# A hybrid DeltaNet and RG-LRU layer on one core: one convolution of the last rest as products on TensorE, the output tiles' third load moved into the last scan, the opening on four strips

## The reference, cut to what matters

```python
shift, scale, gate = split(silu(c) @ ada_w + ada_b)          # the "mod" row, 3 x 1024, one for prompt, one for sample
h    = rmsnorm(x, pre_w) * (1 + scale) + shift
proj = h @ w_in                                              # q, k, v, z, beta, a, rx, rg
q, k, v = silu(short_conv(qkv, conv_w))                      # 4 taps along the tokens
o    = gated_delta(q, k, v, g, beta, s0)                     # both directions, chunks of 64, 8 heads of 128
o    = rmsnorm(o_f + flip(o_b), norm_w) * silu(z)
xf   = short_conv(rx, conv_w) + conv_b                       # 8 blocks of 128
r, i = sigmoid(xf @ w_r + b_r), sigmoid(xf @ w_i + b_i)
y_rg = (scan(a, bx) + flip(scan(a, bx))) * silu(rg)
y    = concat(o, y_rg) @ w_out                               # 1152 x 2048 @ 2048 x 1024
out  = x + gate * rmsnorm(y, post_w)                         # also the final states of the prompt
```

## Time and profile before

| | |
|---|---|
| Time, median of 3 runs | 1277.43 us (1277.24 to 1278.47) |
| The profiled execution | 1277.96 us, of which the span of the trace is 1276.3 us |
| PE busy | 1200.8 us, 94% of the span, 8626 instructions |
| DVE busy | 988.7 us, 77% |
| ACT busy | 727.7 us, 57% |
| POOL busy | 134.5 us, 11% |
| Mean granted TensorE clock | 0.983 of full speed (1.2 and 2.4 GHz are its two levels) |
| Costliest group | the projection's products L800 to L802, 1176 each, 428.5, 397.5 and 397.8 us of busy PE |
| Output products | L1165, 756 in all, 297 us |

### The profile page before, as it was taken

One profiled execution on the slowest core, in us unless ns is written; L12 is line 12 of the kernel. 1 busy time (PEld: TensorE's weight loads), 2 busy tenths in 40 slices (PEclk: granted clock), 3 DMA queues, 4 the chain that ended last, 5 costly groups with the idle time before them and its releaser, 6 DMA issues.

```text
span 1276.3 us, 23925 instructions
## 1 busy us (share of the span) xinstructions
PE 1200.8 (94%) x8626; PEld 1070.7 (84%) x8626; DVE 988.7 (77%) x2033; ACT 727.7 (57%) x1721; POOL 134.5 (11%) x138
## 2 busy tenths in 40 slices
PE   5999999999999999999999999999998698499997
PEld 2699989998999899899989998998898375288885
DVE  5774998999899989999998999898999757422221
ACT  4745487648665874777486658656775736111110
POOL 4000010101010100011010101000100000412120
PEclk9999999999999999999999999999999799799999
DMA  8522111112011211211121112112112902443330
GB/s 292 167 59 72 34 60 47 37 52 80 26 52 58 67 36 41 87 30 53 52 76 30 52 39 86 36 34 64 60 52 82 380 22 83 136 122 101 107 115 33
DMA packets 96431, 99.25 MB, mean 78 GB/s; under 512 B 4497, under 2 KB 79522, under 8 KB 96322
## 3 DMA queue, kind: packets, MB, share of 16 engines
q1 hardware_dynamic: 93378, 87.33, 22.3%
q0 software_dynamic: 2944, 10.49, 2.2%
HBM read 82.50 MB, written 15.30 MB: 77 GB/s over the span
## 4 chain that ended last, share of the span: by engine, by line
PE 48%; DVE 34%; issue 10%; ACT 5%; DMA 1%; DVEq 1%; SPq 0%; POOL 0%; ACTq 0%; POOLq 0%
PE bank L1165 12%; DVE arena L1938 6%; DVE arena L1936 6%; PE bank L800 5%; PE bank L801 5%; PE bank L802 5%; DVE arena L1777 4%; PE bank L1025 3%; DVE w_lo L1656 2%; DVE arena L1903 2%; PE bank L1139 2%; PE bank L1151 2%; PE bank L1072 2%; PE bank L1112 2%; PE bank L1121 2%
## 5 line engine op out<-in xcount | busy, mean ns | idle before, releaser
L800 PE MATMUL bank<-hT_hi,w_hi 128*128 128x384 f32 (+1 forms) x1176 | 428.5, 364 | 1.8 <-DVE w_lo L1656 1.2
L802 PE MATMUL bank<-hT_hi,w_lo 128*128 128x384 f32 (+1 forms) x1176 | 397.8, 338 | 0.0
L801 PE MATMUL bank<-hT_lo,w_hi 128*128 128x384 f32 (+1 forms) x1176 | 397.5, 338 | 0.0
L800 PEld LDWEIGHTS bank<-hT_hi,w_hi 128*128 128x128 f32 x1176 | 222.2, 189 | 11.1 <-DVE w_lo L1656 2.7
L801 PEld LDWEIGHTS bank<-hT_lo,w_hi 128*128 128x128 f32 x1176 | 222.2, 189 | 5.1
L802 PEld LDWEIGHTS bank<-hT_hi,w_lo 128*128 128x128 f32 x1176 | 221.2, 188 | 0.0
L1777 DVE SCALAR_TENSOR_TENSOR arena<-arena 128x1154 f32<-128x1154 f32 x96 | 141.1, 1470 | 5.2 <-DVE arena L1777 2.8
L1520 ACT ACTIVATE arena<-bank,arena 128x128 f32<-128x128 f32 x272 | 78.2, 370 | 104.2 <-PE bank L1129 104.2
L1165 PE MATMUL bank<-wo_hi,ot_hi 128*128 128x512 f32 x252 | 99.8, 396 | 22.5 <-DVE ot_lo L2145 16.7
L1165 PE MATMUL bank<-wo_hi,ot_lo 128*128 128x512 f32 x252 | 98.6, 391 | 0.0
L1165 PE MATMUL bank<-wo_lo,ot_hi 128*128 128x512 f32 x252 | 98.6, 391 | 0.0
(11 more groups left out here) (246 smaller groups left out, 2223.7 us busy)
## 6 DMA issues: line engine op xcount, KB each, us to landing
w_raw<-w_in SPq DMA_DIRECT2D x49, 512.0 KB, 4.0
arena<-scr_G SPq DMA_DIRECT2D x16, 576.0 KB, 4.7
arena<-x_sample SPq DMA_DIRECT2D x16, 512.0 KB, 7.6
arena<-ada_w SPq DMA_DIRECT2D x16, 512.0 KB, 10.9
wo<-w_out SPq DMA_DIRECT2D x4, 2048.0 KB, 13.0
ot<-scr_o SPq DMA_DIRECT2D x7, 1024.0 KB, 6.5
scr_o<-arena POOLq DMA_DIRECT2D x8, 576.0 KB, 3.7
scr_o<-arena POOLq DMA_DIRECT2D x8, 512.0 KB, 2.9
```

Source lines behind the costliest of these rows:

```text
L800: pe.matmul(out, w_hi[:, slot, k], hT_hi[:, k, cols], start=first, stop=False)
L801: pe.matmul(out, w_hi[:, slot, k], hT_lo[:, k, cols], start=False, stop=False)
L802: return pe.matmul(out, w_lo[:, slot, k], hT_hi[:, k, cols], start=False, stop=last)
```

## The change

Five things are done at once.

1. **Opening.** `ada_rows` writes four strips of 256 columns (output partitions 0, 32, 64 and 96) for each k instead of two of 512. DVE and ACT copy two strips each, the transposes use four banks with one more wait (`mod_turned` 6), and `make_mod` has five DVE instructions where it had three. Two of POOL's clears (`sub[0]`, `Z`) now stand behind `baT_made`.
2. **Gate row.** The norm weight is loaded beside the gate row in four small loads and multiplied into it by DVE at step 1 of the last scan (four multiplications of 2 rows x 256). POOL's two multiplications of 128 x 1024 and a load of 512 KB go.
3. **Heads.** The backward scan over the samples runs as one instruction (step 6). The first tap of xf goes from DVE (step 7) to ACT (step 6, Identity with scale and bias); DVE's taps 1 and 2 stand at steps 7 and 8. The two silus stand at steps 5 and 7.
4. **Last rest.** ACT makes four diagonal matrices of v's taps, and PE convolves v by 12 fp32 products in banks 2 to 4; ACT takes the silu from PSUM in three pieces. DVE's three taps go. The norm of o is done by nine ACT copies instead of one DVE instruction, and `turn_o` stands ahead of v's products.
5. **Output.** Tile 2's rows are loaded in the last scan behind tile 1's, its last head's rows with those of tiles 0 and 1, into the space that held tile 0's high part (`ot_raw`, `ot_high` and `ot_low` rotate three buffers). Its high and low part stand ahead of `y_tile(0, 0)`. `raw_last(0)` comes one k earlier, and DVE's copy of the states stands behind its last two `low_wo` instead of ahead of them.

```diff
 def load_o_rows(tile, first, n):
+    to, done = ((ot[:, 0], ot_in[0]), (ot[:, 1], ot_in[1]), (ot_raw[0], ot_next_in))[tile]
...
             load_o_rows(1, 0, HEADS - 1)
+            load_o_rows(2, 0, HEADS - 1)
...
             load_o_rows(1, HEADS - 1, 1)
+            load_o_rows(2, HEADS - 1, 1)
...
-            sp.dma_start(post_b, post_norm_w.to_broadcast([P, D])).then_inc(post_in, 16)
...
             sp.wait_ge(y_made, 1)
             sp.dma_start(y_prompt[0], y_out[:, 0]).then_inc(y_stored[0], 16)
-            load_o(0, 2)
...
-            for s in range(2):
-                gp.tensor_tensor(gate_post[:, s], gate_post[:, s], post_b, ALU.mult).then_inc(gate_post_made, 1)
...
-                for n in range(2):
-                    j = 2 * n + half
-                    mm = pe.matmul(banks[0][32 * j:32 * j + 2, :], silu_c[:, :, k], adaw[:, half, k, 512 * n:512 * n + 512],
+                for j in range(4):
+                    mm = pe.matmul(banks[0][32 * j:32 * j + 2, 0:256], silu_c[:, :, k], adaw[:, half, k, 256 * j:256 * j + 256],
...
+                    project(IN_SCAN + 8, 64 - IN_SCAN, b)
+                    pe.wait_ge(scores_taken.sem, scores_taken.next(b, 28))
+                    turn_o(b)
+                    pe.wait_ge(turn_taken.sem, turn_taken.next(b, 12))
+                    pe.wait_ge(proj_taken.sem, proj_taken.at(b, 6))
+                    pe.wait_ge(conv_done.sem, conv_done.at(b, 3))
+                    pe.wait_ge(v_begun.sem, v_begun.next(b, 4))
+                    for g, (o, n) in enumerate(GROUPS):
+                        for t in range(4):
+                            mm = pe.matmul(banks[2 + g][:, 0:n], v_diag[:, t], raw[:, 1, o + t:o + t + n],
+                                           start=(t == 0), stop=(t == 3))
+                    mm.then_inc(conv_done.sem, 1)
+                    project(72, 16, b)
...
                         if last and step == 1:
-                            pe.wait_ge(gate_row_made, 4)
+                            pe.wait_ge(gate_summed, 4)
...
-                    for k in range(16):
-                        mm = out_product(buf, half, k, k == 0, k == 15)
+                    for k in K_ORDER:
+                        if half == 0 and k == K_LAST[0]:
+                            pe.wait_ge(wo_hi_made, 16)
+                            pe.wait_ge(wo_lo_made, 16)
+                        mm = out_product(buf, half, k, k == K_ORDER[0], k == K_ORDER[-1])
...
-                if i == 10:
+                if i == 9:
                     raw_last(0)
...
+                if final:
+                    act.wait_ge(o_meaned.sem, o_meaned.at(b, 2))
+                    for ch in range(NCH):
+                        last_o = act.activation(o_tok[:, ch], o_tok[:, ch], ACT.Copy, scale=hcc["rstd"][:, ch:ch + 1])
...
-                    if step in (5, 6) and not last:
-                        x = (sz, sg)[step - 5]
+                    if step in (5, 7) and not last:
+                        x = sg if step == 5 else sz
...
+                    if step == 6 and not last:
...
+                        act.activation(xf, raw[:, 0, 0:TW], ACT.Identity, bias=colsB[:, bd(B_CB + b + 1, 1)],
+                                       scale=rconvw[:, 0, bd(b + 1, 1)]).then_inc(xf_begun.sem, 1)
...
-            act.wait_ge(gate_post_made, 2)
+            high_part(0, 2, 64)
             y_tile(0, 0)
-            high_part(0, 2, 80)
...
-                                  (slice(TW - 1, MID - 1, -1), colsB[:, bd(B_ST + 8 + b, 1)]),
-                                  (slice(MID - 1, P + GAP - 1, -1), RC[:, MID:MID + 1]))[d]
+                                  (slice(TW - 1, P + GAP - 1, -1), colsB[:, bd(B_ST + 8 + b, 1)]))[d]
...
-            TAPS = [[], [(1, 0)], [(1, 1)], [(1, 2)], [(1, 3)], [], [], [(2, 0)], [(2, 1)]]
+            TAPS = [[], [(1, 0)], [(1, 1)], [(1, 2)], [(1, 3)], [], [], [(2, 1)], [(2, 2)]]
...
+                    if step == 1 and last:
+                        for j, (row, post) in enumerate(zip(gate_rows, post_rows)):
+                            dve.wait_ge(gate_summed, j + 1)
+                            dve.tensor_tensor(row, row, post, ALU.mult).then_inc(gate_row_made, 1)
...
-            for i in range(5, 12):
-                low_wo(i)
-            dve.wait_ge(states_turned, 1)
-            dve.tensor_copy(hc[0:16, 0:P], banks[7][0:16, 0:P]).then_inc(states_taken, 1)
-            for i in range(12, 14):
+            for i in range(5, 14):
                 low_wo(i)
...
-            dve.wait_ge(gate_post_made, 2)
+            low_part(0, 2)
+            dve.wait_ge(post_in, 16 * 4)
             y_tile(0, 0, 0)
             for i in range(14, 16):
                 low_wo(i)
-            low_part(0, 2)
+            dve.wait_ge(states_turned, 1)
+            dve.tensor_copy(hc[0:16, 0:P], banks[7][0:16, 0:P]).then_inc(states_taken, 1)
             y_tile(1, 1, 1)
```

178 lines of the change are left out of this document (103 added, 75 removed).

## The result

| | before | after |
|---|---|---|
| Time, median | 1277.34 us (1277.10 to 1278.47) | 1256.12 us (1255.92 to 1257.22), 4 runs each |
| Ratio | | 0.9834 (95%: 0.9821 to 0.9846) |
| Span of the trace | 1276.3 us | 1254.3 us |
| PE busy | 1200.8 us, 94% | 1199.7 us, 96% |

The change makes the kernel 21.2 us faster by the medians. PE's busy time is nearly the same in sum: the strips shorten `ada_rows` from 14.8 to 9.2 us, and v's products add 7.9. So what is gained in all came out of waits. I tracked it by the start of the same PE instruction in both traces: each term is the shift that builds up across its stretch.

A forecast was written before the change was run, and what follows sets the result against it. PE, busy 94% of the span, was taken as the bound, so savings count where it waits. Opening -2.0, gate row 0, heads -0.6, last rest +4.0 and output -19.5 sum to -18.1: 1259.3 us, range 1250 to 1266.

The forecast's parts named there:

- What bounds the kernel: Whole kernel: PE is full nearly everywhere, so savings count where PE waits; the chain's 34% for DVE doesn't describe the heads.
- Opening, -2.0: Opening: four strips shorten `ada_rows`, cut short by the last load's landing at 47.3 to 49.2; -2.0 us, bounds -3.4 and -1.
- Gate row, 0: Last scan: DVE's four multiplications and SP's row stores cost nothing; 0 us, POOL's saved 6.16 us counted in the output.
- Heads, -0.6: Seven heads: DVE's lighter step 7 gains only tenths, -0.1 us each; -0.6 us, bounds -6 and +2.4.
- the 0.4 that the prediction named as its own limit: Inner heads: the forecast is wrong if heads differ from 118.36 us by over 0.4 us.
- step 6 loses what step 7 wins, because the longer backward scan stands there in one piece: Heads: the one-piece scan at step 6 cancels step 7's gain from losing the 0.88 us tap; -0.1 us per head taken.
- The statement on the joins: Head joins: relieving DVE gains only tenths at PE's 0.40 us wait, since DVE then waits 0.50 us for ACT's scaling of q.
- Last rest, +4.0: Last rest: v's products delay the gate products and ACT's chain behind them by 7.7 us; +4.0 us, bounds -3.4 and +6.
- The rival in which DVE bounds the last rest: Last rest: DVE's release decides, giving -3.4 us instead of +4; 1251.9 us, chance 0.15.
- Output, -19.5: Output: the 16.70 us wait before tile 2, 1.6 ahead of it and 1.2 of restart go; -19.5 us, bounds -20.5 and -13.
- The slack at `y_made` 1: Output: `y_made` 1 ends near 1094.4, about 1 us before PE needs it; the shared port could use that up.
- The sum: Whole kernel: -2.0 + 0 - 0.6 + 4.0 - 19.5 = -18.1 us, from 1277.43 to 1259.3 us, chance 0.58.

The follow-up runs named there:

- the run with the late load: Changed kernel with tile 2 loaded behind `y_made` 1 again and its high and low parts behind the first `y_tile`: 1272.54 us.

## Why the prediction was right, and where it was wrong

- **What bounds the kernel.** Right in the main: what is gained in all came from PE's waits, with PE's busy time 1.1 us less, and the chain's 34% for DVE were no measure of the heads. But the small waits in the heads were worth more than the prediction gave them.
- **Opening, -2.0.** Right in mechanism: the landing is the bound (48.1, between the 47.3 and 49.2 of the prediction). The products end 2.98 us earlier (2.3 forecast), at 49.17 instead of 52.15, of which 0.40 are lost again by 75.61 (0.3 forecast). The four strips do run side by side (1.05 us for two k). The run with two strips gives the part 2.9 us. One sum is wrong without effect: 3.4 us is four times 0.84, the gain of one half's eight k, and both halves would give 6.7 if PE alone decided.
- **Gate row, 0.** Right for the row itself; its worth is in the output.
- **Heads, -0.6.** Wrong: -3.65, 0.61 for each of six heads, inside the term's bounds, but past the 0.4 that the prediction named as its own limit. The step that failed is "step 6 loses what step 7 wins, because the longer backward scan stands there in one piece". Step 6 loses nothing: PE has other work there and no wait in the trace, and the tap was not what mattered. The one-piece scan takes the second piece (0.87 us) out of step 7, behind which PE waited. Runs: one piece brings 0.96 us a head with the tap on ACT (118.73 to 117.77), and 0.54 with it on DVE (118.36 to 117.82), of which 0.31 + 0.10 are the wait at step 8; the tap's move brings 0.05 with one piece and -0.37 with two. The two comparisons with the kernel before, 118.36, hold the moved silus as well; they were not tried alone. The statement on the joins held: a wait of 0.40 us for DVE only changed its place, from ahead of the first block of 32x32 products (409.18) to ahead of the second (409.13 in the changed kernel). The 79.60 us of ACT are of a whole head, and not of its scan as the text reads.
- **Last rest, +4.0.** Right, against the trace's own naming of DVE. The gate products came 7.76 us later by the shift (7.7 forecast), and 1.53 by the clock instead of about 5, since the heads had given more; DVE's transposes ended 3.8 earlier (3.4 forecast) and PE had nothing of that; the scaling of u waited for ACT. On the clock of the trace of before the 64x64 products came at 1010.6 (1009.2 to 1010.9 forecast). Two details were missed: the 32x32 products do not start with DVE but wait for ACT's squares of q, and 1.08 us of the term is the wait for "issue", without which it would be +3.6. The rival in which DVE bounds the last rest falls by the run without the part, which is faster, not slower.
- **Output, -19.5.** Right: -20.46. The wait of 16.70 and the 1.59 ahead of it are gone, tile 2's first product starts under the last raw product's tail (0.56), and the restart gives 1.14 (seven products take 2.00 us from 1093.37, instead of 3.14). That is 19.99; the other 0.5 us were not followed. The slack at `y_made` 1 was 2.1 us and not 1, since the first `y_tile` began at the end of DVE's low part, not behind POOL, and took 3.48 us (1087.79 to 1091.27) instead of the 4.3 taken. The port that the Trainium skill names ("SBUF — State Buffer", section "SBUF: two separate sides") took nothing of it: POOL's additions began only 0.35 us before the first `y_tile` ended. Where they do lie side by side, the rows agree with the rule: in the run with the late load POOL's additions begin at 1091.04, and DVE's addition, which begins at 1091.20, takes 2.20 us instead of 1.23.
- **The sum.** -18.1 against -22.0: heads -3.05, output -0.96, opening -0.58, last rest +0.69. The measured 1256.12 us lies in the range, but that is luck in part: its lower end was drawn for a last rest that DVE bounds (1251.9), which did not come, and only so had it room for the miss in the heads.

## What to carry to other kernels

A wait names what came last, not what decides: before you relieve an engine, look at when the next one on the path ends (here ACT, 1.5 us before DVE), and keep work that can wait out of the way of the instruction that starts that chain: with 16 projection units behind the first gate products instead of ahead of them, the hole in the last rest was gone. A part that costs time in one order can be in the faster kernel in another: with v's products the kernel was 2.9 us slower as they were placed, and 2.25 us faster once these units and the next late thing (a load, 9.2 us) had been moved as well. In a chain with full and empty steps, count the longest step, not the sum: one long instruction in a step where the other engine has work was better than two pieces, the second of which stood where it waited.
